# Last projection of a decoder layer: Strassen on every second weight slab instead of every third, with two of the four sums of weight blocks made by accumulating transfers

## The reference, cut to what matters

```python
# x (256, 2048) float32, after the mixers
x = _layer_norm(DEEPNORM_ALPHA * x + mix, ln1_gain, ln1_bias)
h = jnp.square(jax.nn.relu(x @ w_ff1)) @ w_ff2     # w_ff1 2048 x 8192, w_ff2 8192 x 2048
x = _layer_norm(DEEPNORM_ALPHA * x + h, ln2_gain, ln2_bias)
```

## Time and profile before

| what | value |
|---|---|
| time, median of 3 runs | 1241.91 us (1241.68 to 1242.8) |
| the profiled execution's own time | 1241.83 us |
| its span, first to last instruction | 1240.0 us |
| granted TensorE clock, mean | 0.999 |
| PE busy | 1218.8 us, 98% of the span |
| PEld busy (weight loads of PE, beside the matmuls) | 1031.9 us, 83% |
| DVE busy | 861.9 us, 70% |
| ACT busy | 619.6 us, 50% |
| POOL busy | 137.5 us, 11% |
| transfers | 222.38 MB, mean 179 GB/s, none issued by GpSimd |

### The profile page before, as it was taken

One profiled execution on the slowest core, in us unless ns is written; L12 is line 12 of the kernel. 1 busy time (PEld: TensorE's weight loads), 2 busy tenths in 40 slices (PEclk: granted clock), 3 DMA queues, 4 the chain that ended last, 5 costly groups with the idle time before them and its releaser, 6 DMA issues.

```text
span 1240.0 us, 22985 instructions
## 1 busy us (share of the span) xinstructions
PE 1218.8 (98%) x9585; PEld 1031.9 (83%) x9585; DVE 861.9 (70%) x909; ACT 619.6 (50%) x674; POOL 137.5 (11%) x94
## 2 busy tenths in 40 slices
PE   8999999999999999999999999999999999999996
PEld 8888888888779778888888888888888888888884
DVE  5688887465766375765455555545689998899987
ACT  6754555545666254453434343343455555566651
POOL 0022112000000000055000000000122221022220
PEclk9999999999999999999999999999999999999999
DMA  9454465332421156635555555555565555555541
GB/s 339 150 210 170 172 252 189 104 138 104 170 103 54 54 215 234 242 110 196 192 180 201 174 200 177 195 186 186 199 245 203 202 203 204 188 208 200 200 155 68
DMA packets 34206, 222.38 MB, mean 179 GB/s; under 512 B 4717, under 2 KB 5101, under 8 KB 8782
## 3 DMA queue, kind: packets, MB, share of 16 engines
q1 hardware_dynamic: 34126, 221.21, 50.2%
HBM read 219.10 MB, written 2.10 MB: 178 GB/s over the span
## 4 chain that ended last, share of the span: by engine, by line
PE 55%; DVE 1%; ACT 0%; issue 0%; ACTq 0%; DVEq 0%
PE ps L531 55%; DVE stats L2139 0%; DVE xres L2136 0%; DVE wlo_end L2301 0%; DVE xres L2329 0%; DVE xres L2327 0%; ACT whi_end L1283 0%; DVE xres L2317 0%; ACT xres L1283 0%; DVE xres L2321 0%; ACT shi L1283 0%; DVE moments L2142 0%; PE ps L1175 0%; DVE moments L2149 0%; ACT moments L1283 0%
## 5 line engine op out<-in xcount | busy, mean ns | idle before, releaser
L1712 DVE TENSOR_TENSOR wlo<-stage,whi 128x2048 fp32r<-128x2048 f32 x166 | 387.2, 2333 | 245.7 <-ACT whi L1283 244.9
L531 PE MATMUL ps<-acts,whi 128*128 128x512 f32 (+1 forms) x1728 | 535.0, 392 | 3.4 <-DVE wlo L1739 2.1
L1283 ACT ACTIVATE whi<-stage 128x2048 fp32r<-128x2048 f32 (+2 forms) x196 | 361.9, 1848 | 308.7 <-PE ps L531 303.9
L531 PEld LDWEIGHTS ps<-acts,wlo 128*128 128x128 f32 x1680 | 315.8, 188 | 72.5
L531 PE MATMUL ps<-acts,wlo 128*128 128x256 f32 x1680 | 334.8, 278 | 0.0
L531 PEld LDWEIGHTS ps<-acts,whi 128*128 128x128 f32 x1728 | 264.0, 189 | 8.0 <-DVE wlo L1739 2.3
L531 PE MATMUL ps<-whi,shi 128*128 128x512 f32 x402 | 110.9, 389 | 0.6 <-issue 0.6
L531 PE MATMUL ps<-whi,slo 128*128 128x512 f32 x402 | 110.8, 389 | 0.0
L531 PE MATMUL ps<-wlo,shi 128*128 128x512 f32 x402 | 110.8, 389 | 0.0
L1283 ACT ACTIVATE shi<-hid 128x512 fp32r<-128x512 f32 x64 | 40.5, 632 | 124.1 <-PE ps L531 124.1
L531 PEld LDWEIGHTS ps<-whi,shi 128*128 128x128 f32 x402 | 75.3, 188 | 16.5 <-issue 1.0
(11 more groups left out here) (290 smaller groups left out, 1394.6 us busy)
## 6 DMA issues: line engine op xcount, KB each, us to landing
stage<-w_ff SPq DMA_DIRECT2D x128, 1024.0 KB, 4.8
stage<-w_in SPq DMA_DIRECT2D x48, 1024.0 KB, 4.9
stage<-w_out SPq DMA_DIRECT2D x16, 1024.0 KB, 4.9
stage<-w_in SPq DMA_DIRECT2D x6, 512.0 KB, 9.4
xstage<-xT SPq DMA_DIRECT2D x4, 512.0 KB, 7.4
TM_TT<-eyes SPq DMA_DIRECT2D x4, 512.0 KB, 7.7
xres<-x SPq DMA_DIRECT2D x1, 2048.0 KB, 9.6
gain<-ln_gain SPq DMA_DIRECT2D x2, 1024.0 KB, 7.3
```

The costliest lines, as they stand in the source:

```text
L531: return pe.matmul(out, lhsT, rhs, start=start, stop=stop, skip_group_check=True)
L1283: return act.activation(out, in_, func, **kw)
L1712: TTn(wlo[k0 % NHL][:, :], stage[k0 % NST][:, :], f(whi[k0 % NHL][:, :]), ALU.subtract).then_inc(s_lo, 1)
```

## The change

Every second slab becomes a quad: 4, 6, ..., 28 (13) and 37, 39, ..., 59 (12), in all 25 where there were 17. The first two sums of weight blocks are no longer made by DVE. GpSimd issues two transfers for each quad: the first copies two blocks of 128 x 512 from HBM to `tsum`, the second adds a third block to both (`accum_op`). There are two `tsum` buffers, used in turn, the second in the space of the later `bias2`. The loads of `gain2` and `bias2` therefore move behind the last slab. ACT rounds the sums of a quad that follows another at distance two in the quad's own step, no longer one slab before. The split of the hidden values comes first for all slabs but the last; for slab 63 the weight's parts come first, and `shared_taken(1, 2)` goes behind them. The loads of two small weights at the start report to a semaphore that existed already.

```diff
-QUADS = (tuple(range(4, 29, 3)), tuple(range(38, 60, 3)))
+QUADS = (tuple(range(4, 29, 2)), tuple(range(37, 60, 2)))
-        tsum = at("tsum", 12, [P, 4, 512])
+        tsums = [at("tsum0", 12, [P, 4, 512]), at("tsum1", 9, [P, 4, 512])]
 # SP
-            slabs(G_FF2, 0, 2, t["w_ff2"])
-            sp.wait_ge(s_used, G_FF2)
+            slabs(G_FF2, 0, DFF // P // 4, t["w_ff2"])
+            sp.wait_ge(s_ql, 2 * len(QUAD))
             sp.dma_start(gain2[:, :], ...
             sp.dma_start(bias2[:, :], ...
-            slabs(G_FF2, 2, DFF // P // 4, t["w_ff2"])
 # PE, start of the kernel
-            pe.wait_ge(s_cst, 16)
-            pe.wait_ge(s_lup, 32)
+            pe.wait_ge(s_cst, 48)
 # ACT
-                act.wait_ge(s_qs, 3 * k + 3)
-                A(thi[:, :, :], tsum[:, :, :], ACT.Copy).then_inc(s_qh, 1)
+                act.wait_ge(s_qs, 2 * k + 2)
+                A(thi[:, :, :], tsums[k % 2][:, :, :], ACT.Copy).then_inc(s_qh, 1)
             for n in range(1, LAST_PAIR + 2):
                 if n in QUAD:
                     split(hid[:, 2 * m:2 * m + 2, :], g, None, n % 2)
+                    if n - 2 in QUAD:
+                        quad_sums_hi(n)
                     hi_own(g)
                 elif n == LAST_PAIR + 1:
                     act.wait_ge(s_used, G_FF2 + QUAD[-1] + 1)
-                    split(hid[:, 2 * m:2 * m + 2, :], g, None, n % 2)
                     A(whi_end[:, :], stage[g % NST][:, :], ACT.Copy).then_inc(s_hi, 1)
+                    split(hid[:, 2 * m:2 * m + 2, :], g, None, n % 2)
-                if n + 1 in QUAD:
+                if n + 1 in QUAD and n - 1 not in QUAD:
                     quad_sums_hi(n + 1)
 # DVE, quad_sums
+                elif k > 1:
+                    dve.wait_ge(s_ql, 2 * k - 2)
                 dve.wait_ge(s_stage[g % NST], 16 * (g // NST + 1))
-                TTn(tsum[:, 0:2, :], src[:, 1::2, :], src[:, 0:1, :].broadcast_to([P, 2, 512]), ALU.add).then_inc(s_qs, 1)
-                dve.wait_ge(s_qs, 3 * k + 1)
+                dve.wait_ge(s_lsum, 32 * k + 32)
                 TTn(tsum[:, 2, :], tsum[:, 0, :], src[:, 3, :], ALU.add).then_inc(s_qs, 1)
 # DVE, the loop over slabs
-                if n in QUAD:
+                if n in QUAD and n - 2 not in QUAD:
                     quad_sums_lo(n)
-                if n >= 4:
+                if n <= LAST_PAIR:
                     split(pair_of_hidden(n), n, n % 2, g - 1)
                 if n in QUAD:
+                    if n - 2 in QUAD:
+                        quad_sums_lo(n)
                     lo_own(g)
                 elif n == LAST_PAIR + 1:
                     dve.wait_ge(s_hi, g + 1)
                     TTn(wlo_end[:, :], ...).then_inc(s_lo, 1)
+                    split(pair_of_hidden(n), n, n % 2, g - 1)
+                    shared_taken(1, 2)
-                if 1 <= after < 4:
+                if 1 <= after < 4 and n != LAST_PAIR:
                     shared_taken(sweep(n), after - 1)
 # POOL
+            def sums_begun(k):
+                if k:
+                    pool.wait_ge(s_lsum, 32 * k)
+                if k == len(QUADS[0]) + 1:
+                    pool.wait_ge(s_pd, 8)
+                w = t["w_ff2"][QUAD[k]].rearrange("p (j q) -> p j q", j=4)
+                pool.dma_start(tsums[k % 2][:, 0:2, :], w[:, 1::2, :]).then_inc(s_lsum, 16)
+            def sums_ended(k):
+                w = t["w_ff2"][QUAD[k]].rearrange("p (j q) -> p j q", j=4)
+                pool.wait_ge(s_lsum, 32 * k + 16)
+                pool.dma_start(tsums[k % 2][:, 0:2, :], w[:, 0:1, :].broadcast_to([P, 2, 512]), accum_op=ALU.add
+                               ).then_inc(s_lsum, 16)
+            pool.wait_ge(s_lnp, 8)
+            sums_begun(0)
+            sums_ended(0)
             pool.wait_ge(s_ff, N_FF1)
             for k, n in enumerate(QUAD):
                 if k:
                     pool.wait_ge(s_ql, 2 * k)
+                if k + 1 < len(QUAD):
+                    sums_begun(k + 1)
                 PT(asum[:, 0:2, :], ...)
                 PT(asum[:, 2, :], ...)
                 PT(asum[:, 3, :], ...)
+                if k + 1 < len(QUAD):
+                    sums_ended(k + 1)
```

More of the change, by code:

```diff
@@ L254, in build @@
         s_cst, s_pos, s_attc, s_levc, s_gup = (
-            sem("consts_loaded"), sem("positions_loaded"), sem("attention_consts_loaded"),
+            sem("constants_and_lora_weights_loaded"), sem("positions_loaded"), sem("attention_consts_loaded"),
             sem("level_masks_loaded"), sem("gate_up_loaded"))
@@ L259, in build @@
         s_vecl, s_lncol = sem("vectors_loaded"), sem("ln1_columns_loaded")
-        s_vec, s_lup = sem("zeros_then_vectors_ready"), sem("lora_weights_loaded")
+        s_vec, s_lsum = sem("zeros_then_vectors_ready"), sem("block_sums_loaded")
         s_lora, s_z, s_sig = sem("lora_activated"), sem("decay_logits"), sem("decay_sigmoid")
@@ L465, in _ @@
             slab_half(2, 1)
-            sp.dma_start(wup[:, :], t["w_up"]).then_inc(s_lup, 16)
-            sp.dma_start(aup[64:128, :], t["a_up"]).then_inc(s_lup, 16)
+            sp.dma_start(wup[:, :], t["w_up"]).then_inc(s_cst, 16)
+            sp.dma_start(aup[64:128, :], t["a_up"]).then_inc(s_cst, 16)
             sp.dma_start(cst[:, :], t["consts"][:, 0:C_SMALL]).then_inc(s_cst, 16)
@@ L1668, in shared_copied @@
                 act.wait_ge(s_ql, 2 * quads_to(h))
-                A(tsum[:, 0, :], ps[:, shared_bank(h, 0), :], ACT.Copy).then_inc(s_qh, 1)
+                A(tsums[0][:, 0, :], ps[:, shared_bank(h, 0), :], ACT.Copy).then_inc(s_qh, 1)
             for n in range(1, LAST_PAIR + 2):
                 g, m = G_FF2 + n, n % (DFF // P // 2)
-                if n == 4:
-                    act.wait_ge(s_ff, N_FF1)
+                if n <= 4:
+                    act.wait_ge(s_ff, n + 1 if n < 4 else N_FF1)
                 if n in QUAD:
                     split(hid[:, 2 * m:2 * m + 2, :], g, None, n % 2)
+                    if n - 2 in QUAD:
+                        quad_sums_hi(n)
                     hi_own(g)
@@ L2243, in quad_sums @@
                 src = stage[g % NST][:, :].rearrange("p (j q) -> p j q", j=4)
+                tsum = tsums[k % 2]
                 if k == 0:
                     dve.wait_ge(s_ff, N_FF1)
-                    dve.wait_ge(s_lnp, 8)
-                else:
-                    dve.wait_ge(s_ql, 2 * k)
+                elif k > 1:
+                    dve.wait_ge(s_ql, 2 * k - 2)
                 dve.wait_ge(s_stage[g % NST], 16 * (g // NST + 1))
-                TTn(tsum[:, 0:2, :], src[:, 1::2, :], src[:, 0:1, :].broadcast_to([P, 2, 512]), ALU.add).then_inc(s_qs, 1)
-                dve.wait_ge(s_qs, 3 * k + 1)
+                dve.wait_ge(s_lsum, 32 * k + 32)
                 TTn(tsum[:, 2, :], tsum[:, 0, :], src[:, 3, :], ALU.add).then_inc(s_qs, 1)
-                dve.wait_ge(s_qs, 3 * k + 2)
+                dve.wait_ge(s_qs, 2 * k + 1)
                 TTn(tsum[:, 3, :], tsum[:, 2, :], src[:, 2, :], ALU.add).then_inc(s_qs, 1)
@@ L2261, in quad_sums_lo @@
                 dve.wait_ge(s_qh, rounded_count(n, 1))
-                TTn(tlo[:, :, :], tsum[:, :, :], f(thi[:, :, :]), ALU.subtract).then_inc(s_ql, 1)
+                TTn(tlo[:, :, :], tsums[k % 2][:, :, :], f(thi[:, :, :]), ALU.subtract).then_inc(s_ql, 1)
                 dve.wait_ge(s_qh, rounded_count(n, 2))
@@ L2268, in shared_taken @@
                 top, right, bottom, corner = (xres[:, a, quarter(2 * h + q)] for a, q in ((0, 0), (0, 1), (1, 0), (1, 1)))
-                copied, v, z = (tsum[:, i, :] for i in range(3))
+                copied, v, z = (tsums[0][:, i, :] for i in range(3))
                 p1, p5, p7, p6 = (ps[:, shared_bank(h, i), :] for i in range(4))
```

5 lines of the change are left out of this document (removed).

## The result

The changed kernel takes 1320.71 us (median of 6 runs, 1318.12 to 1324.54) where the kernel before took 1243.15 in the same comparison. The ratio is 1.063, 95% interval 1.060 to 1.065. It is slower by 78 us. The forecast was 1235.7, with a range up to 1256, and 0.65 for faster. Rival B happened, far above the 1252 of its first case: the time lies between its 1282 (a chain of 12.2 us) and its 1355 (15.4 us).

What follows compares the result with a forecast made beforehand. PE was taken as the bound, with DVE next. Matmuls -5.4, DVE stalls +1.2 and the end -2.0 gave -6.2 us against 1241.83, 1235.6, stated as 1235.7 us; range 1233.0 to 1256.

Steps and rivals of the forecast that it cites:

- Rival B: At `sums_begun`, waiting for the previous quad's landing: two transfers in series exceed 10.20 us and become the bound; chance 0.26.
- first case: Rival B with landings of 4.8 and 6.1 us: period 10.9 us, +16 us, 1252 us.
- step 1: Last projection, PE: 8 more quads, each 3 matmuls shorter, take 5.44 us off while PE stays the bound.
- Step 3, the transfers: GpSimd's two transfers per quad: chain of 9.6 us (bounds 6.8 to 15.4) fits under 10.20 us and costs nothing.
- Step 3, the throughput: A pair of slabs asks for 308 GB/s, or 360 counting the buffer's reading, under the 426 of the densest stretch.
- Step 2, DVE: DVE needs 9.74 us per pair against PE's 10.20; stalls of 0.05 us in 23 intervals, +1.2 us.
- Rival C: DVE becomes the bound through POOL: 0.3 to 0.6 us in 23 intervals, +6 to +13 us, 1241 to 1247; chance 0.12.
- Step 4, the end: Slabs 62 to 63: the `wlo_end` stall and restart go, 2.47 us; POOL's moved multiplications cost 0.5; net -2.0 us.
- the sign that the prediction named: Sign that step 4 is wrong: a period of 10.2 us with PE waiting for `slo` of slab 63.

Runs made afterwards that it cites:

- first-transfer-only version without POOL's sums: Changed kernel without the second, adding transfer, and with GpSimd's three sums made for the first quad alone: 1236.75 us, ratio 0.9950.
- first-only version: Changed kernel without the second, adding transfer, GpSimd's three sums kept: 1244.56 us, ratio 1.0000.
- both repairs: Changed kernel with copies on SyncE's queue, three buffers, each copy a period earlier, the adding transfer ahead of POOL's sums: 1257.73 us, ratio 1.0109.

## Why the prediction was wrong

- **What bounds the kernel, step 1.** Right. The first-transfer-only version without POOL's sums shows the 5.4 us in full.
- **Step 3, the transfers.** This is the step that failed: the chain was put at 9.6 us, fitting under 10.20 and costing nothing. "2 x 4.8 = 9.6 us" took the slab load of the earlier trace rows as the nearest row for both. The first transfer came out near it (4.5 us). The second landed in 8.4 us, and the chain from first issue to next first issue is 14.4 us: 5.8 to the second issue (the landing, or POOL's three sums, which end 5.3 us behind the first issue, whichever is later), 8.0 to the landing, 0.6 until POOL goes on. The sums were taken at 3.4 us and take 4.5 here. The row chosen has double the bytes, and that was counted on to cover the reading of the buffer; it covers neither that (2.1 us) nor the second place (0.5 to 1.1 us). The upper bound of 15.4 held, the value taken was near the lower one, and the range of the time stopped at a chain of 11.1.
- **Step 3, the throughput.** Also wrong. 360 GB/s against 426 counted bytes. By shares of all engines, a plain slab is 0.57 x 15.64 / 3 = 3.0 us, the copy 1.5 us (0.72 of 10.4 us in the first-only version, less 6.0), and the adding transfer about 3.1 us (0.88 of some 12 us with the copy on SyncE's queue, less 7.5). These are estimates from the shares of the windows. Together they give 10.6 us for a pair of 10.2. An adding transfer costs about twice a copy of its size, and twice was not in my sum. By this estimate overlap alone could not have brought the period to 10.2; both repairs together, at a share of 0.96, agree, though DVE's own rows were as long there.
- **Step 2, DVE.** The order and the place of the stall were right, the size was not. I had 9.74 us for a pair and 1.2 us of stall in all. With the landings out of the way DVE's starts are 10.23 and 10.74 us apart, without POOL's sums PE runs free; the term measured 7.3 us. My row for `lo_own` showed the loss of one meeting: 0.55 us, 2.30 against 1.75 by durations; the 1.66 beside 2.30 was a distance of starts. With an issue of 0.72 us put ahead of them, POOL's sums start later, and meet L2247, L2249 and `slo` in its place (1.23, 0.83, 0.94 in the first-only version, 0.94 us more than free). The later start is not what makes it dearer: with all sums by DVE and no issue ahead, they meet `lo_own`, L2250 and L2252 and cost 0.94 us too. At this density DVE has no pause beside POOL's last sum, which took 0.46 us before and takes 1.32 there. Rival C's place and price, 6 to 13 us, fit this; it was hidden under B.
- **The two rules that were cited.** That a DVE instruction with two inputs in SBUF contends with POOL instructions that read SBUF and not with those that only write it (the Trainium skill, "SBUF — State Buffer", "Who interferes with whom") agrees with both halves, if an issue is taken as an instruction that only writes: the issues without sums left `lo_own` at 1.75 us, the sums cost 7.3 us. By an estimate from the fit in the Trainium skill, "DMA: Bandwidth & Descriptors", "Anatomy of one DMA — SWDGE (gpsimd) path", 512 KB take 3.2 us. The shortest landings of transfers issued by GpSimd here are 3.9 us for a copy and 5.8 for an adding transfer, always with slab loads beside them, so in this traffic the measurement decides.
- **Step 4, the end.** The new order was right: 2.47 us forecast, 2.5 and 2.7 measured alone. The multiplications that move beside it were priced too low, at 0.5 us with bounds of 0 and 1.1. In the changed kernel they stretched `wlo` of slab 62 to 3.39 us and PE waited 1.08 us for it. In the two versions with the first transfer alone PE waited 1.71 us for `slo` of slab 63, the sign that the prediction named. Of the net 2.0 us, 1.5 was left in the one without POOL's sums and 0.4 with every third slab.
- **Rival B** had the place (the landing of the quad before) and the point (10.20 us) right. At 14.4 its own rule gives 23 x 4.2 = 97 us on 1235.7; 20 waits were seen, and 1320.7 is 85 us above it. It had 0.26, and it should have had more, since the bounds went from 6.8 to 15.4 and the point lay at 10.2: more than half of that span was on its side.

What stays open: why the second of two plain transfers is slower than the first from the same source (6.3 against 5.8 us, 5.9 against 4.8), and whether capacity, the landing that is left in the loop or DVE beside POOL bounds the version with both repairs.

## What to carry to other kernels

When a chain with an unseen operation must fit under a period, count it link by link against the point where it decides, and let the chance follow how much of the bounds lies beyond it. The nearest row by place is no measure for an operation of another kind. And before work is added for a second-busiest engine, look at what the engine that slows it does at the new times: POOL's sums, which met mainly one DVE instruction before, met four in the changed kernel.

## What the runs showed of the hardware

- An adding transfer of 512 KB into SBUF landed in 5.8 us at best; medians were 7.2 to 8.4 us where no copy ran right behind it, and 10.3 with both repairs. A copy of the same size and source landed in 5.7 to 7.9 in its place, the two-block copy in 3.9 at best. By the windows' shares adding took about twice a copy's share of the transfer engines (an estimate).
- GpSimd took 1.20 us to issue an adding transfer, 0.72 us the same one without adding, 0.75 us the first copy in the changed kernel; SyncE 0.55 us for the copy. DVE's instructions kept their length beside the issues alone (1.75 us for `lo_own` in the version without POOL's sums).
- A copy that GpSimd issued right behind an adding transfer landed after 10.3 us (median), where 4.5 is usual.
- POOL's three sums took 0.94 us a pair from DVE in the first-only version. A 128x128 one took 0.46 us when nothing met it and up to 2.39 us beside DVE.
- Slab loads beside the transfers landed in 6.0 us (median) in place of 4.8 and up to 9.2, in the version with both repairs up to 10.6. No wait of PE, ACT or DVE for a slab load shows in the lists of waits of this stage.
